# Memory attention: the two halves of a head's outputs issued two steps apart instead of four

## The reference

```python
h = rms_norm(x, norm_x[l])
m = rms_norm(mem, norm_mem[l])
q = (h @ xq[l]).reshape(B, S, XATTN_HEADS, XATTN_DH)
k, v = jnp.split(m @ xkv[l], 2, axis=-1)
q = rms_norm(q, xq_gain[l])
k = rms_norm(k, xk_gain[l])
s = jnp.einsum('bshd,bmhd->bhsm', q, k).astype(jnp.float32) * (XATTN_DH ** -0.5)
p = jax.nn.softmax(s, axis=-1).astype(v.dtype)
o = jnp.einsum('bhsm,bmhd->bshd', p, v).reshape(B, S, D)
x = x + o @ xo[l]
```

## Time and profile before

| | |
|---|---|
| median of 3 runs | 1620.7 us (1620.5 to 1621.25) |
| the profiled execution's own time | 1620.83 us |
| its span in the trace | 1618.5 us |
| PE busy | 1563.8 us, 97% of the span |
| DVE, ACT, POOL busy | 64%, 50%, 13% |
| granted TensorE clock, mean over the span | 0.995 of full |

### The profile page before, as it was taken

The page is one execution under the profiler, slowest core; times in us unless marked ns, Lnnn a source line. Parts: engine busy times, 40 slices in busy tenths (PEclk is TensorE's granted clock), DMA queues, the critical chain, the costliest instruction groups (busy, mean ns, idle before and its releaser), DMA issues.

```text
span 1618.5 us, 20084 instructions
## 1 busy us (share of the span) xinstructions
PE 1563.8 (97%) x7908; PEld 1256.6 (78%) x7908; DVE 1038.2 (64%) x1713; ACT 805.2 (50%) x1369; POOL 203.8 (13%) x282
## 2 busy tenths in 40 slices
PE   9999999889999999999989999999999999999998
PEld 8877677667788888888768666878767988888887
DVE  4367967786648989998877787574765333333331
ACT  5277873325444888888864434333333333333220
POOL 1000014440332300000044111111100000000000
PEclk9999999999999999999999999999999999999999
DMA  6122121104526999999853111021122232323232
GB/s 243 55 77 78 53 79 53 47 33 146 214 99 214 310 421 421 422 420 420 322 220 104 53 52 53 27 95 62 53 79 63 94 100 82 104 92 100 82 107 89
DMA packets 78642, 236.20 MB, mean 146 GB/s; under 512 B 6960, under 2 KB 9296, under 8 KB 66256
## 3 DMA queue, kind: packets, MB, share of 16 engines
q1 hardware_dynamic: 68288, 207.91, 35.6%
q10 hardware_dynamic: 6624, 14.88, 2.4%
q0 software_dynamic: 3632, 12.08, 2.0%
HBM read 222.26 MB, written 12.60 MB: 145 GB/s over the span
## 4 chain that ended last, share of the span: by engine, by line
PE 79%; DVE 13%; ACT 4%; issue 2%; DMA 1%; POOL 1%; SPq 0%; DVEq 0%; ACTq 0%; POOLq 0%
PE bank L106 76%; PE bank L109 4%; DVE low L131 2%; DVE REST L121 2%; ACT REST L112 2%; DVE REST L134 1%; DVE REST L131 1%; ACT CHH L115 1%; DVE REST L143 1%; DVE low L121 1%; DVE AL L121 1%; DVE R L131 1%; DVE REST L127 1%; DVE REST L140 1%; DVE st L137 1%
## 5 line engine op out<-in xcount | busy, mean ns | idle before, releaser
L121 DVE TENSOR_TENSOR low<-slot,CHH 128x1024 fp32r<-128x1024 f32 (+1 forms) x300 | 297.3, 1033 | 113.8 <-ACT CHH L115 112.7
L115 ACT ACTIVATE CHH<-slot 128x1024 fp32r<-128x1024 f32 (+1 forms) x300 | 258.8, 901 | 130.7 <-PE bank L106 65.9
L131 DVE SCALAR_TENSOR_TENSOR low<-slot,smalls,CHH 128x512 fp32r<-128x512 f32 (+1 forms) x232 | 170.0, 762 | 191.8 <-ACT CHH L115 191.6
L106 PE MATMUL bank<-AH,CHH 128*128 128x512 f32 (+1 forms) x640 | 250.4, 391 | 0.2 <-DVE AL L121 0.2
L106 PE MATMUL bank<-AL,CHH 128*128 128x512 f32 (+1 forms) x640 | 243.5, 381 | 0.0
L106 PE MATMUL bank<-AH,low 128*128 128x512 f32 (+1 forms) x640 | 243.4, 380 | 0.0
L115 ACT ACTIVATE CHH<-slot,smalls 128x512 fp32r<-128x512 f32 (+1 forms) x232 | 154.7, 701 | 136.5 <-PE bank L106 67.7
L106 PE MATMUL bank<-CHH,AH 128*128 128x512 f32 x512 | 216.3, 422 | 4.4 <-ACT REST L115 2.5
L106 PE MATMUL bank<-low,AH 128*128 128x512 f32 x512 | 200.9, 392 | 0.0
L106 PE MATMUL bank<-CHH,AL 128*128 128x512 f32 x512 | 200.3, 391 | 0.0
L106 PE MATMUL bank<-CHH,XTF 128*128 128x512 f32 x512 | 161.3, 396 | 1.8 <-DVE REST L118 1.0
(11 more groups left out here) (177 smaller groups left out, 2350.5 us busy)
## 6 DMA issues: line engine op xcount, KB each, us to landing
slot<-in_w_in SPq DMA_DIRECT2D x35, 1024.0 KB, 5.2
slot<-in_w_exp_gate SPq DMA_DIRECT2D x32, 1024.0 KB, 13.2
slot<-in_w_exp_up SPq DMA_DIRECT2D x32, 1024.0 KB, 13.3
slot<-in_w_exp_down SPq DMA_DIRECT2D x32, 1024.0 KB, 13.7
slot<-in_w_gate SPq DMA_DIRECT2D x10, 1024.0 KB, 5.1
slot<-in_w_up SPq DMA_DIRECT2D x10, 1024.0 KB, 5.1
slot<-in_w_down SPq DMA_DIRECT2D x10, 1024.0 KB, 5.0
slot<-in_w_out SPq DMA_DIRECT2D x8, 1024.0 KB, 5.0
```

What stands on the lines that cost most here:

```text
L106: return self.e.matmul(out, l, r, start=start, stop=stop) if self.e else Issued()
L115: return self.e.activation(out, in_, ACT.Copy, scale=scale) if self.e else Issued()
L121: return self.e.tensor_tensor(out, a, b, op) if self.e else Issued()
L131: return self.e.scalar_tensor_tensor(out=out, in0=a, scalar=s, in1=b, op0=op0, op1=op1) if self.e else Issued()
```

## The change

A new constant `XA_HALF` = 2 takes the place of `XA[3]` = 4 in the pause between the two halves of a head, on PE, ACT and DVE alike. The pause before the first half stays at 4. The outputs then stand after these dense steps: xo(0,0) 60, xo(0,1) 62, xo(1,0) 64, xo(1,1) 66; xo(2,0) 92, xo(2,1) 94, xo(3,0) 96, xo(3,1) 98. The instructions are the same in kind and number, and so are the banks and the order in which the "op" bank is taken.

```diff
--- before.py
+++ after.py
@@ -43,6 +43,7 @@
 HG_LAST = 1, 1, 1, 5
 XA = 2, 3, 3, 4, 5, 4
 XA_AT = 22
+XA_HALF = 2
 RD = 6
 RT = 8, 3, 6, 6, 2
 RT_GATE = 22, 16, 10, 4
@@ -1346,7 +1347,7 @@
                                   c == 0, c == 1)
                 m.then_inc(*mark("pe_xa", ("xo", h, d)))
                 if d == 0:
-                    yield from pause(XA[3])
+                    yield from pause(XA_HALF)
 
         xa_gen = staggered([xa_item(h, i) for h, i in xa_items], XA[4], XA[5], XA[5] - 1)
         w3 = pe.stepping(chain(banks_for("three"), *(seg_turned(f"xq{n}", h2, rows_of("n3"), lambda i, n=n: q_turn(n, i), rows=True) for n in range(2)),
```

## The result

| | before | changed |
|---|---|---|
| median of 12 runs | 1619.22 us (1617.7 to 1621.25) | 1615.65 us (1614.34 to 1617.34) |
| ratio | | 0.9978, 95% interval 0.9969 to 0.9986 |
| profiled execution: own time, span | 1620.83, 1618.5 us | 1615.63, 1613.3 us |

The change made the kernel faster by 3.6 us (the interval is 2.3 to 5.0 us), against a forecast of 4.3. The two profiled spans stand 5.2 us apart.

What follows compares the result with a forecast made beforehand. The chain is mostly PE, so time is won only where PE waits or runs slowly. Gains of 3.34 us (first pair) and 1.00 (second), say 4.3, from 1620.7 give 1616.4 us; range 1615.0 to 1618.9.

Steps and rivals of the forecast that it cites:

- Where PE loses time: PE waits at 1170 to 1232 us: 2.8 and 1.5 us for subtractions freeing the output bank, the change's target.
- The price of a turn of the bank: Output bank: an unhindered half holds it 3.38 us; the next waits by that less PE's work between their starts.
- First pair: xo(0,0) to step 69: gain 3.34 us, from 2.97 + 1.64 less new waits of 0.05, 0.17 and 1.11.
- the wait for the tp bank: Between qt(1,2) and xt(3,0), no longer covered by xo(1,1): a new wait of 1.11 us.
- Second pair: Outputs of heads 2 and 3: gain 1.00 us, from 1.66 less waits of 0.06 and twice 0.30.
- The mis-sized term: At xo(1,0): the long wait is followed by PE at 1.2 GHz, costing 1.64 us more, all counted as gain.
- the clock that still falls in the changed kernel: Rival: short waits in the changed stretch still make the clock fall once; gain 2.7 us, time 1618.0, chance 0.13.
- The time itself: Whole kernel: 1620.7 - 4.3 = 1616.4 us, chance 0.63.
- The own time: Profiled execution of the changed kernel: own time 1616.5 us, with a span of 1614.2.
- The rule on short waits: PE clock: short idle stretches between matmul groups taking PSUM banks in turn can alone make it fall and rise again.
- Slower: Rival: DVE falls behind PE, 1.37 us for each of five tight gaps; 2.6 us slower, time 1623.3, chance 0.05.
- given back by a queue: Rival: ACT or DVE order adds 0.6 to 0.75 us at five tight gaps; gain about 1.0 us, chance 0.12.

Runs made afterwards that it cites:

- one step: The changed kernel with XA_HALF = 1 instead of 2; timed ratio to before 0.9992 (0.9983 to 1.0001).
- Three steps: The changed kernel with XA_HALF = 3 instead of 2; timed ratio to before 0.9982 (0.9973 to 0.9991).
- The two qt-in-op kernels: The changed kernel and the kernel before, each with transpositions qt(1,2) and qt(1,3) in bank op instead of tp; ratios to before 0.9959 and 1.0001.
- before again: The kernel before, profiled and timed a second time with no edit; ratio to before 1.0002 (0.9993 to 1.0011).
- second pair only: The kernel before with the two-step distance for heads 2 and 3 only; ratio to before 0.9992 (0.9983 to 1.0001).
- before with qt in op: The kernel before with transpositions qt(1,2) and qt(1,3) in bank op instead of tp; ratio to before 1.0001 (0.9990 to 1.0011).
- the last two kernels: Changed kernel with qt(1,2), qt(1,3) in op and xo(2,1), xo(3,1) in zp banks, 1612.17 us; and the changed kernel again, unedited, 1616.26 us.
- its first pair alone: The kernel before with the two-step distance for heads 0 and 1 only; ratio to before 0.9984 (0.9975 to 0.9993).
- its version with qt in op: The changed kernel with transpositions qt(1,2) and qt(1,3) in bank op instead of tp; ratio to before 0.9959 (0.9946 to 0.9973).

## Why the prediction was right, and what was mis-sized

- **Where PE loses time**: right. The two waits named there are gone, and behind the first output nothing else moved with the change: the section between the pairs by 0.03 and the end by 0.01 us.
- **The price of a turn of the bank, 3.38 us**: right, measured 3.29 to 3.47 where it binds (3.29 and 3.30 in one step, 3.37 to 3.47 in the changed kernel). Three steps and one step show its limit: it grows (3.73, 4.59 us) when the copy or subtraction lands behind other work.
- **First pair**: 3.34 us forecast, 3.31 measured. xo(0,1) had no wait (0.05 forecast), xo(1,0) none, xo(1,1) started 3.44 us after xo(1,0) (3.50 forecast), and the wait for the tp bank was 0.94 us recorded, 1.11 from start to start, to the hundredth the value read at qt(1,3). The two qt-in-op kernels show that the wait is for this bank, and that xo(1,1) between the two had covered it.
- **Second pair**: 1.00 forecast, 1.00 measured. Its parts moved a little: no wait before xo(2,1) (0.06 forecast), and 0.37 and 0.27 us instead of twice 0.30, by the starts against the 3.10 of PE's own work.
- **The mis-sized term**: "The wait of 2.97 us has drawn 1.64 us more behind it", and the sum took this 1.64 as part of every execution of the kernel before. Of four profiled executions with that wait unfilled (before, before again, second pair only, before with qt in op) the clock fell in two. Against an execution whose clock held, the change wins 18.22 - 16.60 = 1.62 us in the first pair and 1.00 in the second, 2.62 in all; the fall is worth 19.91 - 18.22 = 1.69 us more, in the part of executions that have it. Half of them would give 3.5 us, and 3.6 was measured, but the interval of 2.3 to 5.0 us holds every share from none to all. That the fall comes only in part of the executions is shown by the four profiles; how large the part is stays open. The clocks of the timed runs don't settle it either: on the chip of the last two kernels, before and changed had the same mean, 0.9975 and 0.9973. I took a single profile for the kernel's rule, and the prediction had as a rival only the clock that still falls in the changed kernel, not the one that often doesn't in the old.
- **The time itself**: 1616.4 us forecast, 1615.65 measured, and that it came so close is in part luck. The forecast stood on a median of 3 runs, 1620.7 us, where 12 runs gave 1619.22: a start 1.5 us too high and a gain 0.7 us too large (4.3 against 3.6) partly cancel.
- **The own time** of the profiled execution: 1616.5 us forecast, 1615.63 measured. The missing 0.87 us lies ahead of the first output, where the change does nothing. There too the clock falls at different places in different executions, in the profile of before near 316, 477 and 497 us, in that of the changed kernel near 316, 484 and 832 us.
- **The rule on short waits** (the Trainium skill, TensorE: Matmul & The Clock Gate, A second HAM failure mode: psum-queue depth-cycling): in the stretch of the change the rule did not hold. The row of waits of at most 0.94 us did not bring the clock down in either profile of the changed kernel, nor in that of its first pair alone. Elsewhere the clock did fall behind waits that short, as the last section shows, so the forecast was right for this stretch, and size alone doesn't make a wait harmless.
- **Slower** and **given back by a queue**: not at two steps. At one step the second is real: the first pair takes 2.5 us more than with two steps, 1.0 of it over what the bank's price alone would take, though it struck one gap and not each of them.

## What to carry to other kernels

A single bank passed between engines has a price per turn that can be read off a trace (write, copy, subtract, release); the uses should be spaced by that price, no closer and not two in one place. Before work is moved out of a place, look at which wait it was covering, for that wait is what comes next; here it took 1.1 of the 5.4 us to be had, and giving the transpositions the other bank won it back, and as much again at qt(1,3). And a fall of the clock seen in one profile is an event with a chance, to be weighted and not added.

## What was not expected of the hardware

Behind one and the same wait PE's clock can fall to the lower level (1.2 GHz) in one execution and hold in the next, far from the change as well. At about 315 us the changed kernel and its version with qt in op have equal waits of 2.5 us. Wait and window, first of the changed kernel:

```profile
315.16 1.16 PE L107 MATMUL bank<-REST 64*128 64x128 f32 x16 [2.52 <-DVE REST L144]
```

```profile
316.00:320.00 4.00, 3.82 (x17) 2.64 (x15) 2.76 (x4) 1.11 (x2) 2.80 (x4) 0.59 0.01 4
```

and then of its version with qt in op:

```profile
315.74 1.16 PE L107 MATMUL bank<-REST 64*128 64x128 f32 x16 [2.53 <-DVE REST L144]
```

```profile
316.00:320.00 4.00, 3.47 (x29) 2.65 (x28) 2.80 (x4) 1.40 (x3) 3.39 (x5) 1.00 0.01 4
```

A long wait isn't needed for it. In the profile of the kernel before, the clock fell near 477 us with no recorded wait of more than 0.55 us in the 10 us before, but with 16 narrow matmuls (20 columns) behind that wait:

```profile
473.75 1.93 PE L106 MATMUL bank<-REST,TT 128*128 128x20 f32 x16 [0.55 <-ACT TT L115]
```

```profile
477.00:480.00 3.00, 3.00 (x12) 2.60 (x12) 1.25 (x2) 1.69 (x4) 0.00 (x0) 0.50 0.33 139
```

In the same kernel profiled again the same place, with a wait of 0.56 us, kept its clock:

```profile
477.00:480.00 3.00, 3.00 (x18) 2.37 (x16) 1.32 (x3) 2.37 (x5) 0.57 (x2) 1.00 0.38 158
```

What decides between the two is open: no run here varied it.

Over the span the kernel before had mean granted clocks of 0.994 to 0.998 and the changed one of 0.995 to 1.000 in their timed runs, with the quicker runs of the changed one mostly at the higher clock (1614.34, 1614.45 and 1614.48 us at 1.000 against 1617.34 at 0.995). So these falls go with part of the scatter of 3 us between runs of one and the same kernel.
